# Gated levels 0 to 4 of a bidirectional linear-attention stage: both directions in one product over crossed operands

## The reference, cut to what matters

```python
b = jnp.cumsum(log_f, axis=2)
decay = jnp.exp(jnp.where(causal, b[:, :, :, None] - b[:, :, None, :], NEG))
A = jnp.einsum('bnthd,bnshd,bntshd->bnhts', q, k, decay)      # per direction, with its own k and log_f
...
s_f, ST_f = _hgrn2_dir(q_h, k_f, v_h, lf_f, S0[:, 0])
s_b, ST_b = _hgrn2_dir(flip(q_h), flip(k_b), flip(v_h), flip(lf_b), S0[:, 1])
```

## Time and profile before

| | |
|---|---|
| median of three runs | 739.67 us |
| lowest of them | 735.71 us |
| span of the profiled execution | 735.1 us |
| PE busy | 682.8 us (93%) |
| DVE busy | 575.1 us (78%) |
| ACT busy | 433.0 us (59%) |
| the stage of the change: diagonal to level 7 | about 134.8 to 220.3 us of the span |

### The profile page before, as it was taken

The page is one execution under the profiler, slowest core; times in us unless marked ns, Lnnn a source line. Parts: engine busy times, 40 slices in busy tenths (PEclk is TensorE's granted clock), DMA queues, the critical chain, the costliest instruction groups (busy, mean ns, idle before and its releaser), DMA issues.

```text
span 735.1 us, 12593 instructions
## 1 busy us (share of the span) xinstructions
PE 682.8 (93%) x4850; PEld 550.1 (75%) x4850; DVE 575.1 (78%) x838; ACT 433.0 (59%) x605; POOL 57.0 (8%) x88
## 2 busy tenths in 40 slices
PE   4699999999899999999997999999999999999981
PEld 2587998898689899954457878888888888888740
DVE  2639998898994367675398998999999999999775
ACT  1637866363232455650034579888888888888731
POOL 2060000000011010132000500000000000000220
PEclk9699999999999999999998999999999999999996
DMA  9989596645767699989626799999999999999242
GB/s 334 387 234 326 192 344 233 226 144 196 279 233 257 210 389 361 333 298 292 202 75 229 290 399 399 398 400 398 400 398 400 398 400 399 399 398 398 76 169 86
DMA packets 91508, 220.07 MB, mean 299 GB/s; under 512 B 3335, under 2 KB 3631, under 8 KB 91455
## 3 DMA queue, kind: packets, MB, share of 16 engines
q1 hardware_dynamic: 85200, 200.29, 74.2%
q0 software_dynamic: 5840, 18.94, 7.6%
q10 hardware_dynamic: 415, 0.14, 0.1%
HBM read 179.99 MB, written 39.36 MB: 298 GB/s over the span
## 4 chain that ended last, share of the span: by engine, by line
PE 73%; DVE 17%; DMA 3%; ACT 3%; issue 2%; SPq 1%; DVEq 0%; ACTq 0%
PE ps L1175 70%; DMA ring<-in_w_in 3%; PE ps L1593 2%; DVE w_lo L1756 2%; DVE arena L1911 1%; DVE arena L1910 1%; PE ps L1612 1%; DVE arena L1856 1%; DVE w_lo L2217 1%; ACT w_hi L829 1%; DVE arena L2103 1%; DVE arena L2084 1%; DVE arena L2311 1%; DVE arena L2313 1%; DVE arena L2109 1%
## 5 line engine op out<-in xcount | busy, mean ns | idle before, releaser
L2217 DVE TENSOR_TENSOR w_lo<-arena,w_hi 128x1024 fp32r<-128x1024 f32 x96 | 114.6, 1220 | 8.6 <-ACT w_hi L1059 7.4
L2217 DVE TENSOR_TENSOR w_lo<-ring,w_hi 128x1024 fp32r<-128x1024 f32 x92 | 109.9, 1220 | 8.9 <-ACT w_hi L1059 8.0
L1059 ACT ACTIVATE w_hi<-arena 128x1024 fp32r<-128x1024 f32 x96 | 101.0, 1064 | 14.9 <-PE ps L1175 14.7
L1059 ACT ACTIVATE w_hi<-ring 128x1024 fp32r<-128x1024 f32 x92 | 96.8, 1063 | 19.7 <-PE ps L1175 19.3
L1175 PE MATMUL ps<-h_hi,w_lo 128*128 128x384 f32 x288 | 101.5, 352 | 7.3 <-DVE w_lo L1756 5.2
L1175 PE MATMUL ps<-w_hi,slot_tokens_lo 128*128 128x512 f32 x256 | 102.7, 401 | 1.2 <-DVE w_lo L2217 1.1
L1175 PE MATMUL ps<-w_hi,slot_tokens_hi 128*128 128x512 f32 x256 | 100.2, 392 | 0.0
L1175 PE MATMUL ps<-w_lo,slot_tokens_hi 128*128 128x512 f32 x256 | 99.7, 390 | 0.0
L1175 PE MATMUL ps<-h_hi,w_hi 128*128 128x384 f32 x288 | 97.2, 338 | 0.0
L1175 PE MATMUL ps<-h_lo,w_hi 128*128 128x384 f32 x288 | 97.2, 337 | 0.0
L1756 DVE TENSOR_TENSOR w_lo<-ring,w_hi 128x1024 fp32r<-128x1024 f32 x44 | 53.6, 1225 | 22.4 <-ACT w_hi L829 21.4
(11 more groups left out here) (373 smaller groups left out, 1114.1 us busy)
## 6 DMA issues: line engine op xcount, KB each, us to landing
slot_rows<-arena SPq DMA_DIRECT2D x12, 2048.0 KB, 18.6
ring<-in_w_in SPq DMA_DIRECT2D x11, 2048.0 KB, 10.2
ring<-in_w_ada SPq DMA_DIRECT2D x10, 2048.0 KB, 8.9
ring<-in_w_up SPq DMA_DIRECT2D x8, 2048.0 KB, 14.7
arena<-in_w_up SPq DMA_DIRECT2D x8, 2048.0 KB, 14.9
ring<-in_w_down SPq DMA_DIRECT2D x8, 2048.0 KB, 10.9
arena<-in_w_gate SPq DMA_DIRECT2D x8, 2048.0 KB, 15.2
arena<-in_w_down SPq DMA_DIRECT2D x8, 2048.0 KB, 11.7
```

The lines of the kernel that those rows point to most:

```text
L1059: act.activation(w_hi[:, at_ % 4, :], raw[:, q * QUARTER:(q + 1) * QUARTER], ACT.Copy).then_inc(S["hi_ready"], 1)
L2217: tt(w_lo[:, at_ % 4, :], raw[:, q * QUARTER:(q + 1) * QUARTER], w_hi[:, at_ % 4, :].bitcast(F32), ALU.subtract).then_inc(S["lo_dve"], 1)
```

## The change

One PE job, one `take` and one `scale` per level serve both directions. The backward queries' left halves and the forward queries' right halves of each block are read as one crossed operand; likewise forward keys left and backward keys right. ACT copies the crossed keys into a contiguous unit KC before each of levels 0 to 4 (`merge`), since the stationary operand of the product is read from there; the moving operand is read through the crossed view. `scale` works for all levels 0 to 6 over both directions in three instructions: keys first (which releases `hg_keys` for the merge), then queries, then the gate products. The list of jobs is reordered, the two directions' masks are added on POOL, and the load of gi_bias moves to another place in the arena and behind `gates_taken`.

```diff
-        return [("take", lv, d), ("scale", lv, d)]
+        return [("take", lv), ("scale", lv)] + ([("merge", lv + 1)] if lv < 4 else [])
...
+    steps += [("merge", 0), ("diag",), ("ada_row", 6), mq[2], ("diag_take",), ("ada_col", 6), ("level", 0), mq[3]] + gated(0)
+    steps += [("lru_act", 2), ("floor",), ("mod", 6), mk[0]]
+    steps += [("level", 1), mk[1]] + gated(1) + [("lru_den", 2), mk[2], ("lru_act", 3), ("ada_row", 7)]
+    steps += [("level", 2), mk[3]] + gated(2) + [("lru_sqrt", 2), ("ada_col", 7), gi[0], ("mod", 7)]
+    steps += [("level", 3), gi[1]] + gated(3) + [("lru_scan", 2), gi[2]]
+    steps += [("level", 4), gi[3]] + gated(4)
+    steps += [("ada_row", 8), ("level", 5), ("tok_take", "gi"), ("ada_col", 8), ("scale", 5), mv[0], ("lru_den", 3), ("lru_sqrt", 3), mv[1], ("mod", 8), ("lru_scan", 3)]
...
+        gi_bias = unit(12, 0, 512)
+        KC = unit(15)
...
+        def crossed(left, right, h, off=0, n=U):
+            step = right - left + h
+            v = arena[:, left + off:left + off + 2 * step].rearrange("p (g x) -> p g x", g=2)[:, :, 0:n]
+            return v.rearrange("p g (b x) -> p b g x", x=2 * h)[:, :, :, 0:h]
+        def crossed_q(h, off=0, n=U):
+            return crossed(0, 4 * U, h, off, n)
+        def crossed_k(h, off=0, n=U):
+            return crossed(U, 2 * U, h, off, n)
+        def block_decay(at_f, at_b, h):
+            v = arena[:, 5 * U + at_f:5 * U + at_f + 2 * (U + at_b - at_f)].rearrange("p (g x) -> p g x", g=2)
+            v = v[:, :, 0:U - h:2 * h]
+            if at_b:
+                v = v[:, ::-1, :]
+            return v.rearrange("p g b -> p b g").unsqueeze(3).broadcast_to([P, U // (2 * h), 2, h])
...
+            half = LEVELS * 32
+            pool.tensor_tensor(masks_wide[:, 0:half], masks_wide[:, 0:half], masks_wide[:, half:2 * half], ALU.add)...
+            pool.tensor_copy(hg_masks.rearrange("p l t -> p (l t)"), masks_wide[:, 0:half])...
+            pool.wait_ge(S["gates_taken"], 4 * C)
+            pool.dma_start(gi_bias, ...)
...
+                elif kind == "merge":
+                    lv = job[1]
+                    act.wait_ge(S["hg_keys"], lv + 1)
+                    if lv == 0:
+                        act.wait_ge(S["gates_taken"], 4 * C)
+                    h = 1 << lv
+                    dst = KC.rearrange("p (b x) -> p b x", x=2 * h).rearrange("p b (g w) -> p b g w", g=2)
+                    act.activation(dst, crossed_k(h), ACT.Identity).then_inc(S["kc_ready"], 1)
...
+            def crossed_blocks(out, lv):
+                for i in range(NT):
+                    for h in range(H):
+                        x = 32 * (H * i + h)
+                        for j in range(4):
+                            t0 = h * T + i * P + 32 * j
+                            last = mm(out[32 * j:32 * j + 32, x:x + 32], KC[:, t0:t0 + 32], crossed_q(1 << lv, t0, 32))
+            def hg_level(lv):
+                pe.wait_ge(S["hg_fwd"], lv + 1)
                 if lv < 5:
-                    blocks(hg_bank(), ((KBF, QFF), (KBB, QFB))[d]).then_inc(S["hg_scores"], 1)
+                    pe.wait_ge(S["kc_ready"], lv + 1)
+                    crossed_blocks(hg_bank(), lv).then_inc(S["hg_scores"], 1)
...
-                        m = hg_masks[:, job[2], lv, :].unsqueeze(1).broadcast_to([P, NT * H, 32])
+                        m = hg_masks[:, lv, :].unsqueeze(1).broadcast_to([P, NT * H, 32])
...
-                    for q, kb, f, right_q in ((QFF, KBF, FF, 1), (QFB, KBB, FB, 0)):
-                        if lv < 5 and right_q == job[2]:
-                            continue
...
+                    step(tt(crossed_k(h), crossed_k(h), block_decay(h, 0, h), ALU.mult), "hg_keys")
+                    step(tt(crossed_q(h), crossed_q(h), block_decay(0, h, h), ALU.mult))
+                    both = arena[:, 5 * U:7 * U]
+                    step(tt(both[:, 0::2 * h], both[:, 0::2 * h], both[:, h::2 * h], ALU.mult), "hg_fwd")
```

More of the change, by code:

```diff
@@ L70 @@
 FIRST_EXPERT = 24
-TOP_BANK = 11
-TOP_SCORES = 15
+TOP_BANK = 6
+TOP_SCORES = 10
 ZERO_AFTER = {4: 1, 6: 1, 8: 1, 15: 2}
@@ L121, in schedule, with gated @@
     steps += [mq[0], ("prep", 1, 0), ("prep", 1, 1), ("lru_mm", 3), mq[1], ("prep", 1, 2), ("prep", 1, 3), ("qfb",)]
-    def gated(lv, d):
-        return [("take", lv, d), ("scale", lv, d)]
[L126 to L132, removed]
+    def gated(lv):
+        return [("take", lv), ("scale", lv)] + ([("merge", lv + 1)] if lv < 4 else [])
[6 more added lines that the diff above has]
+    steps += [("ada_row", 8), ("level", 5), ("tok_take", "gi"), ("ada_col", 8), ("scale", 5), mv[0], ("lru_den", 3), ("lru_sqrt", 3), mv[1], ("mod", 8), ("lru_scan", 3)]
     steps += [("level", 6), mv[2], ("scale", 6), ("take", 6), mv[3], ("tok_take", "mv")]
@@ L359, in build @@
         mv_bias = unit(14, 512, 512)
-        gi_bias = unit(15, 1024, 512)
+        gi_bias = unit(12, 0, 512)
+        KC = unit(15)
         gate_w = unit(3, 1280, 128).rearrange("p (k g) -> p k g", k=KD)
@@ L367, in build @@
         SCX = unit(12, 0, 1024).rearrange("p (d h t) -> p d h t", d=2, h=H)
-        hg_masks = unit(12, 1024, 112).bitcast(U8).rearrange("p (d l t) -> p d l t", d=2, l=LEVELS)
+        hg_masks = unit(12, 1024, 56).bitcast(U8).rearrange("p (l t) -> p l t", l=LEVELS)
         SC32 = unit(12, 1136, 384).rearrange("p (x t) -> p x t", t=32)
@@ L684, in _ @@
             pool.dma_start(m0_cols, a["state_mlstm_m"][0, 0].rearrange("d h -> (d h)").partition_broadcast(P)).then_inc(S["mini_in"], 16)
-            pool.dma_start(gi_bias, a["b_in"][0, WIN_COL["gi"] * G:(WIN_COL["gi"] + 1) * G].partition_broadcast(P)).then_inc(S["gi_bias_in"], 16)
             wide = masks_wide.rearrange("p (x t) -> p x t", t=32)
@@ L690, in _ @@
             pool.wait_ge(S["masks_in"], 64)
-            pool.tensor_copy(hg_masks.rearrange("p d l t -> p (d l t)"), masks_wide).then_inc(S["masks_cast"], 1)
+            half = LEVELS * 32
+            pool.tensor_tensor(masks_wide[:, 0:half], masks_wide[:, 0:half], masks_wide[:, half:2 * half], ALU.add).then_inc(S["masks_cast"], 1)
+            pool.wait_ge(S["masks_cast"], 1)
+            pool.tensor_copy(hg_masks.rearrange("p l t -> p (l t)"), masks_wide[:, 0:half]).then_inc(S["masks_cast"], 1)
+            pool.wait_ge(S["gates_taken"], 4 * C)
+            pool.dma_start(gi_bias, a["b_in"][0, WIN_COL["gi"] * G:(WIN_COL["gi"] + 1) * G].partition_broadcast(P)).then_inc(S["gi_bias_in"], 16)
             pool.wait_ge(S["lru_done"], C)
@@ L1221, in hg_mul @@
                 return mm(out, k[:, s:s + P], q[:, t:t + P], start, stop)
[L1223 to L1228, removed]
+            def crossed_blocks(out, lv):
[5 more added lines that the diff above has]
+                            last = mm(out[32 * j:32 * j + 32, x:x + 32], KC[:, t0:t0 + 32], crossed_q(1 << lv, t0, 32))
+                return last
+            def hg_level(lv):
+                pe.wait_ge(S["hg_fwd"], lv + 1)
                 if lv < 5:
-                    blocks(hg_bank(), ((KBF, QFF), (KBB, QFB))[d]).then_inc(S["hg_scores"], 1)
+                    pe.wait_ge(S["kc_ready"], lv + 1)
+                    crossed_blocks(hg_bank(), lv).then_inc(S["hg_scores"], 1)
                     return
@@ L1377, in _ @@
                 elif kind == "diag":
-                    pe.wait_ge(S["hg_start"], 1)
+                    pe.wait_ge(S["hg_keys"], 1)
                     pe.wait_ge(S["gates_taken"], 4 * C)
@@ L1382, in _ @@
                 elif kind == "level":
-                    hg_level(*job[1:])
+                    hg_level(job[1])
                 elif kind == "fin_T":
@@ L1390, in _ @@
                         pe.wait_ge(S["hg_fwd"], LEVELS + 1)
-                        pe.wait_ge(S["hg_bwd"], LEVELS + 1)
                     for h in range(H):
@@ L1868, in _ @@
                     if (d, h) == (0, 0):
-                        dve.wait_ge(S["masks_cast"], 1)
+                        dve.wait_ge(S["masks_cast"], 2)
                     transformed(("gff", "gfb")[d])
@@ L1872, in _ @@
                     step(ts(chunk(f, h), chunk(f, h), om_lb[:, k:k + 1], lb[:, k:k + 1], ALU.mult, ALU.add))
-                    step(ts(chunk(f, h), chunk(f, h), TINY, None, ALU.max), "hg_start" if (d, h) == (1, H - 1) else "dve")
+                    step(ts(chunk(f, h), chunk(f, h), TINY, None, ALU.max), "hg_keys" if (d, h) == (1, H - 1) else "dve")
                 elif kind == "qfb":
                     transformed("gq")
-                    step(tt(QFB, QFF, FB, ALU.mult), "hg_bwd")
+                    step(tt(QFB, QFF, FB, ALU.mult))
                 elif kind == "diag_take":
```

13 lines of the change are left out of this document (1 added, 12 removed).

## The result

The changed kernel takes 748.8 us (median of four runs, 746.3 to 750.2) where the kernel before takes 737.9 (median of four runs, 735.7 to 740.0; twenty more, taken beside the first experiments, gave 737.9 again, 735.2 to 740.9). The median of 739.67 that the prediction started from was that of the first three. The ratio is 1.014, with a 95% interval of 1.011 to 1.018: slower by 1.4%. That is 10.9 us, where the prediction had 9.2 and arrived at 748.9. The profiled execution took 747.7 us, its span is 746.0.

A forecast was written before the change was run, and what follows sets the result against it. PE bounds most of the kernel, DVE the stretch from 174.95 to 220.9 us. Walk 4.1 plus clock losses 2.8 and 2.3 make 9.2 us; 739.7 + 9.2 = 748.9 us, range 737 to 754.

The forecast's parts named there:

- The event to follow: Start of rg's first unit on PE, at 220.94 us before; whatever moves it moves the end one for one.
- First new wait: PE before gi's first unit, until ACT reads ada_col 7 behind merge 3 and lru_sqrt 2: 5.0 us.
- Second new wait: PE before ada_row 8, whose bank waits for gi's token take: 4.3 us.
- The walk: Each engine's job list followed through the stage on the old clock; rg's first unit starts 4.1 us later.
- The clock: PE's granted clock falls after both waits: 2.8 us lost at the first, 2.3 at the second.
- Level 0, bounds 1.8 and 3.3 us: DVE's scaling of level 0's keys and queries through views changing unit at every element; 3.3 us each taken.
- Level groups and matmuls: PE saves one direction, about 0.96 us, at each of five levels, 4.8 us; crossed moving operand costs nothing.
- DVE 4 to 7 us less to do: Net DVE saving from fewer takes and fused scaling, less level 0's dearer views: 4 to 7 us.
- Levels 5 and 6 give back 1.2 us: Fused scaling at these levels recovers 1.2 us of DVE's 5.2 us lateness before rg's first unit.
- Rival 1: Both waits come but the clock stays up or falls once: +4.1 to +6.9 us, 743.8 to 746.6; chance 0.22.
- Rival 2: PE's work sets the stage's end, at most 7.7 us less, to 732.0; half-way outcomes included; chance 0.17.
- Rival 3: Crossed views cost more than strided ones in products, merges and scales: 4 us or more, 753 and up; chance 0.09.

The follow-up runs named there:

- e1: Changed kernel with ada_col 7 moved ahead of merge 3 and lru_sqrt 2: 743.3 us, ratio 1.007 to the kernel before.
- e7: Changed kernel with lru_act 2 and floor put behind mk0, ahead of level 1: 747.9 us, ratio 1.013 to the kernel before.
- e3: e1 with level 5 and gi's token take also put ahead of ada_row 8: 741.2 us, ratio 1.005 to the kernel before.
- e4: Changed kernel with unread 128x128 products keeping PE busy, 18 before gi's first unit, 15 before ada_row 8: 743.6 us, ratio 1.007.
- e5: Changed kernel with level 0's keys and queries scaled by four operations of 768 columns, as before: 746.8 us, ratio 1.011.
- e6: Kernel before with only levels 5 and 6 scaled in operations fused over both directions: 740.0 us, ratio 1.002.
- e10: e9 with lru_sqrt 2 behind mk3's take and lru_scan 2 behind gi's first unit: 734.9 us, ratio 0.996 to the kernel before.
- e8: Changed kernel, all operations kept, job list reordered (ada_col 7, lru_act 2, level 5 and others earlier): 738.0 us, ratio 1.000 to the kernel before.
- e9: e8 with level 0 scaled by four operations of one unit each: 738.2 us, ratio 0.999 to the kernel before.
- e11: Kernel before, unfused, with only the change's later ada_col 7 and ada_row 8 ahead of level 5 and token take: 741.6 us, ratio 1.006.

## Why the prediction was right, point by point

- **The event to follow.** The stage gave 9.8 us of the 10.9 by which the profiled spans differ; 9.2 were predicted for it. Confirmed.
- **The number itself.** That 748.9 meets 748.8 so closely is luck. The loss was 10.9 us where 9.2 were predicted, and the start was 739.7 where four runs, and twenty more, have 737.9: 1.7 too little and 1.8 too much. The predicted loss is right within a sixth.
- **First new wait, 5.0 us, ada_col 7 read behind merge 3 and lru_sqrt 2.** 5.45 us. e1 moved the one job and the wait fell to 1.54; e7 left it in place and moved earlier work, and it stayed at 5.07. Shown, cause included.
- **Second new wait, 4.3 us.** 4.56 us. The releaser is the token take, but e3 shows that the place of ada_row 8 is not its whole cause: with that cured, scale 4 still comes 3.85 us late. The walk had DVE late behind mv's first split, and the rows of DVE agree (7.39 us idle before it). The time was right; of its causes only the part of ada_row 8 was tried by itself.
- **The clock, 2.8 + 2.3.** The fall came after both waits. It cost 1.8 us on gi's unit (6.1 against 4.3) and 2.1 on ada_row 8 and level 5 (4.9 against 2.8): 3.9 where 5.1 were taken. e4 gives 3.8 for both by another way. The price came from the row of 30 to 40 us, where 2.8 us were lost; here the clock was low for part of each wait already (0.66 over 174 to 176, 0.50 over 202 to 204), when there was nothing to slow down.
- **The walk, 4.1 us.** 9.8 less 3.9 is 5.9; e4, without the clock, gives 6.0. The walk was 1.8 us short. The rows show where some of it lies: PE stands 0.95 us in mq3's unit for "issue" and level 0's products last 1.24 instead of 1.03, so that mk3's weights are rounded later; merge 1 lasts 1.68 instead of 1.48; lru_act 2 begins at 152.81 where 151.5 was reckoned, in an execution whose stage began 0.8 earlier. Everything that hangs on ACT from there comes some 2 us late. It is a chance that the clock's 1.2 us too much and the walk's 1.8 too little nearly cancel: the sum was better than its terms.
- **Level 0, bounds 1.8 and 3.3 us, 3.3 taken.** 3.30 and 3.33. The row of 2.0 ns a column was the right neighbour. That it costs the total nothing in this order is shown by e5.
- **Level groups and matmuls, 0.96 us each, crossed moving operand at nothing.** 1.03 us recorded from level 1 on, as before, so nothing; 1.24 at level 0, 0.2 us more. The Trainium skill's 25 ns from start to start ("TensorE: Matmul & The Clock Gate", "Back-to-back issue gap") doesn't hold for these rows either: 96 records in 1.03 us. But the 96 records are 48 products of the kernel; counted so it is 21 ns each, and by the page's figure five levels would have been worth some 6 us, an estimate, and not the 12 of the prediction. The gap between page and trace is smaller than the prediction made it.
- **DVE 4 to 7 us less to do.** 3.5 less, just under.
- **Levels 5 and 6 give back 1.2 us.** The operations do (1.76 us each). e6 shows that in the kernel before only 0.2 us of it reaches rg. In the changed one DVE is late, and whether it arrives there was not tried alone.
- **Rival 1** (the clock stays up) is refuted by the windows at 0.50. **Rival 2** (PE's work sets the end) failed for this order. e10 is one of its half-way outcomes: with ada_col 7 read early and lru_act 2 out of the way, the stage is 2.5 us shorter, of the 7.7 at most. The condition that it named, ada_col 7 read in time, is needed but not enough (e1 meets most of it and stays 5.1 us of stage above the kernel before); that a new order could meet it was not asked. **Rival 3** (crossed views dearer) falls with e5 and with the products' 1.03 us from level 1 on. **Rival 4** (no effect of the fusion) falls with the operations' times, 1.76 us for two of 0.96 and their gaps, and with the result, since it had nothing move.

What stays open: why PE has the "issue" gap of 0.95 to 1.50 us in mq3, three products behind level 0's, in all kernels of the changed kind. The kernels of the old kind have one of 0.30 to 0.85 in front of level 0's first group. No experiment aimed at it. It is worth about 1 us. Nor does any run try an order like e10's with the operations of before, or move mv's first split alone.

## What to carry to other kernels

When two alternating halves are fused, count the wait that the alternation used to hide before you count the instructions that vanish: here the fused operations, with level 0 left apart, are 3.4 us faster than the kernel before in one order (e10) and some 10 us slower in the one that came with them. How much of the 3.4 a new order would have given the old operations was not tried. Walk each engine's list in order up to every small operation that frees something shared; a copy of 0.16 us behind a merge and a square root held up the busiest engine for 5.45 us. And price a long wait of TensorE with the clock that it loses, which here added 3.9 us to some 10 us of waiting; filling the waits with products that nobody reads got that part back (e4); moving the one job shortened the first wait and lost the clock all the same (e1); two of the three new orders kept it at 1.00 (e8, e10), and e9 did not.

## What the runs showed of the hardware

- **The clock falls after shorter waits than expected, and not always.** Behind 1.54 us (e1, e3) and 2.74 us (e11) it fell to 1.2 GHz; behind 2.07 us it stayed at 1.00 in e8 and fell in e9 (0.83 in 170 to 180), and these two kernels differ only at level 0. What decides it, no run shows. After a short wait the first products still run at full speed and the next ones don't. This is e3's PE timeline behind a wait of 1.54 us:

```profile
174.42 0.47 PE L1204 MATMUL ps<-w_hi,h_lo 128*128 128x512 f32 x1 [1.54 <-ACT small L890]
174.73 0.39 PE L1204 MATMUL ps<-w_lo,h_hi 128*128 128x512 f32 x1
...
176.38 0.63 PE L1204 MATMUL ps<-w_lo,h_hi 128*128 128x512 f32 x1
...
179.29 0.39 PE L1204 MATMUL ps<-w_hi,h_hi 128*128 128x512 f32 x1
```

- **What a view costs on DVE.** 768 columns at every other element of one unit take 0.96 us (e5), as neighbouring ones do. 1536 columns that change unit at each element take 3.30 us, at every second element and beyond 1.76. A wider stride is not free: the gate products of level 1, at every fourth element of each unit, take 1.72 us for 768 columns (164.60 above). On ACT the copy of the crossed keys costs 2.21, 1.68 and 1.49 us at levels 0, 1 and 2, and 1.48 at level 3.
